# Rotating keys and queries by transfers, with a new order in the window attention and an earlier fetch of the distances' table

## What is computed

```python
q = rms_norm(q, q_norm); k = rms_norm(k, k_norm)      # per head, gain of 64
q, k = rope(q, positions), rope(k, positions)         # halves of 32: x1*cos - x2*sin, x2*cos + x1*sin
logits = q @ k.T * 64 ** -0.5                         # masked to the last 128 keys
p = softmax over [logits, sink of the head]           # the sink takes part in the sum only
y = (p @ v) @ w_out
```

## Time and profile before

| | |
|---|---|
| median of 3 timed runs | 2091.65 us |
| the profiled execution | 2096.21 us, span 2094.3 us |
| mean granted TensorE clock | 0.995 |
| PE (matmuls) busy | 2067.1 us, 99% |
| PEld (weight loads, beside PE) | 1740.9 us, 83% |
| DVE (VectorE) busy | 1779.1 us, 85% |
| ACT (ScalarE) busy | 1400.0 us, 67% |
| POOL (GpSimd) busy | 59.6 us, 3% |
| moved by DMA | 565.92 MB, 270 GB/s over the span |

### The profile page before, as it was taken

One profiled execution on the slowest core, in us unless ns is written; L12 is line 12 of the kernel. 1 busy time (PEld: TensorE's weight loads), 2 busy tenths in 40 slices (PEclk: granted clock), 3 DMA queues, 4 the chain that ended last, 5 costly groups with the idle time before them and its releaser, 6 DMA issues. The chain is left out here.

```text
span 2094.3 us, 27806 instructions
## 1 busy us (share of the span) xinstructions
PE 2067.1 (99%) x10830; PEld 1740.9 (83%) x10830; DVE 1779.1 (85%) x2358; ACT 1400.0 (67%) x1855; POOL 59.6 (3%) x58
## 2 busy tenths in 40 slices
PE   9999999999999999999999999999999999999999
PEld 8878888878888888888888888879988888778887
DVE  6776768789999999999999999988878888788887
ACT  5654547568888888888888888867745446565544
POOL 0011002001000000000000000000000000000000
PEclk9999999999999999999999999999999999999999
DMA  9537764659999999999999999954446555346552
GB/s 312 181 121 271 233 209 151 219 199 395 394 395 395 395 395 383 385 380 386 371 393 374 388 372 378 394 202 141 144 159 227 196 181 149 81 154 222 183 197 102
DMA packets 291275, 565.92 MB, mean 270 GB/s; under 512 B 13596, under 2 KB 120224, under 8 KB 290896
## 3 DMA queue, kind: packets, MB, share of 16 engines
q1 hardware_dynamic: 284480, 537.13, 71.8%
q0 software_dynamic: 5792, 23.78, 3.1%
q10 hardware_dynamic: 864, 3.15, 0.4%
HBM read 555.10 MB, written 12.59 MB: 271 GB/s over the span
## 5 line engine op out<-in xcount | busy, mean ns | idle before, releaser
L505 DVE TENSOR_TENSOR wl<-raw,wh 128x1024 fp32r<-128x1024 f32 x626 | 756.2, 1242 | 99.9 <-ACT wh L497 95.5
L497 ACT ACTIVATE wh<-raw 128x1024 fp32r<-128x1024 f32 x626 | 640.9, 1053 | 154.1 <-PE psum L542 61.7
L505 DVE TENSOR_TENSOR wl<-arena,wh 128x1024 fp32r<-128x1024 f32 x384 | 456.7, 1222 | 37.6 <-ACT wh L497 32.6
L497 ACT ACTIVATE wh<-arena 128x1024 fp32r<-128x1024 f32 x384 | 403.9, 1062 | 84.7 <-PE psum L542 82.5
L540 PE MATMUL psum<-wh,xhl 128*128 128x512 f32 (+1 forms) x1136 | 449.5, 396 | 1.8 <-DVE wl L505 0.9
L542 PE MATMUL psum<-wh,xhl 128*128 128x512 f32 (+1 forms) x1136 | 441.5, 389 | 0.0
L541 PE MATMUL psum<-wl,xhl 128*128 128x512 f32 (+1 forms) x1136 | 440.6, 388 | 0.0
L532 PE MATMUL psum<-xhl,wh 128*128 128x512 f32 x980 | 349.4, 396 | 0.0
L540 PE MATMUL psum<-wh,yh 128*128 128x512 f32 x752 | 295.6, 393 | 1.0 <-DVE yl L1714 1.0
L542 PE MATMUL psum<-wh,yl 128*128 128x512 f32 x752 | 293.0, 390 | 0.0
L541 PE MATMUL psum<-wl,yh 128*128 128x512 f32 x752 | 292.6, 389 | 0.0
(11 more groups left out here) (455 smaller groups left out, 2078.1 us busy)
## 6 DMA issues: line engine op xcount, KB each, us to landing
arena<-in_moe_g SPq DMA_DIRECT2D x72, 1024.0 KB, 8.8
arena<-in_moe_u SPq DMA_DIRECT2D x72, 1024.0 KB, 8.5
raw<-in_moe_d SPq DMA_DIRECT2D x64, 1024.0 KB, 8.8
arena<-in_moe_d SPq DMA_DIRECT2D x48, 1024.0 KB, 8.3
raw<-in_ff_up SPq DMA_DIRECT2D x48, 1024.0 KB, 5.2
raw<-in_moe_g SPq DMA_DIRECT2D x40, 1024.0 KB, 8.1
raw<-in_moe_u SPq DMA_DIRECT2D x40, 1024.0 KB, 9.2
raw<-in_ff_down SPq DMA_DIRECT2D x24, 1024.0 KB, 5.4
```

What stands on the lines that cost most here:

```text
L497: A.activation(unit_made(s, i)[0], raw_half(s, i), ACT.Copy).then_inc(*s.w_hi.tick(i))
L505: V.tensor_tensor(lo, raw_half(s, i), hi.bitcast(F), SUB).then_inc(*s.w_lo.tick(i))
```

## The change

Four parts. (1) GpSimd fetches the bias table and the one-hot matrix at once, without the wait for the first piece of x; the clock holder after the first piece does two turns instead of three. (2) The rotation is done by transfers between partitions of SBUF: when ScalarE has copied a block to `QB`, it waits for its own copy and issues four DMAs of 32 partitions each (64 KB) that write the swapped halves to `T4`. `rope` is gone from TensorE. Sign and gain are now a column `ROT_GAIN`, made by two one-column matmuls (`rotated_gains`) at the section's beginning, and VectorE's `sines` multiplies the swapped block by this column and the sines, in place. `copied` for the later blocks also waits until the earlier contents are used up. (3) `maxima` can do the small steps of two units together. (4) The order is changed: on TensorE `turned(3)` goes ahead of `sums(1)`; on ScalarE `turned(3)`, the copies `newer` and the high halves move; on VectorE `masked(4)`, `masked(6)`, `rows(0, 1)` go ahead of `scales(1)`, `maxima(4)` and `maxima(6)` ahead of unit 13's low half, `older(7)` and `maxima(5, 7)` ahead of `normal(4, 6)`, and `rows(1, 0)` ahead of `normal(7)`.

```diff
--- before.py
+++ after.py
@@ -320,6 +320,7 @@
     back_in = [sig(f"back{n}_landed", 16) for n in range(4)]
     added_in = [sig(f"added{n}_landed", 16) for n in range(3)]
     added_out, added_back = sig("added_stored", 16), [sig(f"added_back{l}", 16) for l in range(2)]
+    rotated = {(n, i): sig(f"rotated{n}{i}", 16) for n in range(3) for i in range(1 if n == 2 else 2)}
     res_in, ln_in, tz_in, out_done = sig("x_landed", 16), sig("ln_landed", 16), sig("tz_landed", 16), sig("out_landed", 16)
 
     def C(name):
@@ -1086,7 +1087,7 @@
                     if c == 3:
                         i.then_inc(*pe.tick(("unit", u), f"{st}.in{n}"))
                 if (m, c) == (0, 0):
-                    hold_clock(7, 3, STILL[:, 0:P], STILL)
+                    hold_clock(7, 2, STILL[:, 0:P], STILL)
                 if (m, c) == (0, 1):
                     T.wait_ge(*distances_in.of("all"))
                     T.matmul(take(4)[0:4, 0:384], S("relb")[0:32, :], C("oh")[0:32, :], start=True, stop=True
@@ -2921,12 +2922,12 @@
     WP, WPO = [ar(9728 + 512 * n, 4, 128) for n in range(4)], [ar(11776 + 512 * n, 4, 128) for n in range(2)]
     WD = ar(8704, 256)
     NSK = SC[:, 960:976]
-    ROT = [SC[:, 640:768], SC[:, 768:896]]
+    ROT_GAIN = SC[:, 640:642]
     RV, RR, RW1, RW2, RW, RW64 = (SC[:, 448 + 2 * n:450 + 2 * n] for n in range(6))
     LG_BANKS = [(5,), (2, 3), (1,), (6, 7), (0,), (1, 5), (4,), (0, 4)]
     PT_BANK = [5, 6, 1, 7, 1, 0, 5, 4]
     AV_BANK = [[5, 5], [1, 5]]
-    Q_BANKS, RO_BANKS, SS_BANK = {2: (0,), 0: (2, 3), 1: (0, 4)}, {2: (6,), 0: (6, 7), 1: (0, 4)}, {2: 4, 0: 4, 1: 1}
+    Q_BANKS, RO_BANKS, SS_BANK = {2: (0,), 0: (2, 3), 1: (0, 4)}, {2: (6,), 0: (6, 7), 1: (2, 3)}, {2: 4, 0: 4, 1: 1}
 
     def win_at(n):
 
@@ -2971,14 +2972,12 @@
             x.then_inc(*pe.tick(f"wi.ss{n}"))
             empties(SS_BANK[n], (dve, f"wi.ss{n}"))
 
-        def rope(n):
-            for i, b in enumerate(RO_BANKS[n]):
-                take(b)
-                T.wait_ge(*act.of(f"wi.qc{n}{i}"))
-                T.wait_ge(*dve.of("wi.rot"))
-                T.matmul(bk(b), ROT[n == 2], flat(QB[:, 2 * i:2 * i + 2, :]), start=True, stop=True
-                         ).then_inc(*pe.tick(f"wi.ro{n}"))
-                empties(b, (dve, f"wi.ro{n}"))
+        def rotated_gains():
+            ps = take(6)
+            for i, n in enumerate(("aqn", "akn")):
+                x = T.matmul(ps[:, i:i + 1], C("rot"), S(n), start=True, stop=True)
+            x.then_inc(*pe.tick("wi.rot"))
+            empties(6, (dve, "wi.rot"))
 
         def spread_keys():
             ps = take(5)
@@ -3037,16 +3036,15 @@
             x.then_inc(*pe.tick(f"wi.av{g}{t}"))
             empties(b, (dve, f"wi.x{g}{t}"))
 
+        rotated_gains()
         project(2, 0, by_blocks("nm1"))
         project(2, 1)
         project(0, 0)
-        rope(2)
         project(0, 1)
         sums(2)
         project(0, 2)
         project(0, 3)
         spread_keys()
-        rope(0)
         sums(0)
         project(1, 0)
         logits(0, 2)
@@ -3056,12 +3054,11 @@
         project(1, 3)
         turned(0)
         turned(2)
-        rope(1)
         weigh(0, 0)
         turned(1)
         logits(4, 6)
+        turned(3)
         sums(1)
-        turned(3)
         weigh(0, 1)
 
         def turn_first():
@@ -3086,9 +3083,14 @@
         def copied(n, i):
             A.wait_ge(*pe.of(f"wi.p{n}{i}"))
             if n != 2:
-                A.wait_ge(*pe.of(f"wi.ro{0 if n else 2}"))
+                A.wait_ge(*rotated[0 if n else 2, 0].of("all"))
                 A.wait_ge(*dve.of(f"wi.c0{i}" if n else "wi.c20"))
+                A.wait_ge(*dve.of(f"wi.q{0 if n else 2}"))
             A.activation(QB[:, 2 * i:2 * i + 2, :], heads(bk(Q_BANKS[n][i]), 2), ACT.Copy).then_inc(*act.tick(f"wi.qc{n}{i}"))
+            A.wait_ge(*act.of(f"wi.qc{n}{i}"))
+            for a in range(4):
+                A.dma_start(T4[32 * a:32 * a + 32, 2 * i:2 * i + 2, :], QB[32 * (a ^ 1):32 * (a ^ 1) + 32, 2 * i:2 * i + 2, :]
+                            ).then_inc(*rotated[n, i].tick("all"))
 
         def squared(n, i):
             if n != 2:
@@ -3153,24 +3155,22 @@
         squared(1, 1)
         weighed(0, 0)
         turned(1)
+        turned(3)
         hi_to(main, U + 15)
-        turned(3)
-        hi_to(main, U + 16)
         weighed(0, 1)
         hi_to(main, U + 17)
+        newer(5)
         soft(4)
-        newer(5)
+        newer(7)
+        soft(6)
         hi_to(main, U + 18)
-        soft(6)
-        newer(7)
-        hi_to(main, U + 19)
         soft(5)
         turned(4)
         turned(6)
-        hi_to(main, U + 20)
+        hi_to(main, U + 19)
         soft(7)
         weighed(1, 0)
-        hi_to(main, U + 21)
+        hi_to(main, U + 20)
         turned(5)
         turned(7)
         hi_to(main, un["wi.o2"][0] + NU)
@@ -3187,11 +3187,12 @@
                                    CS[:, 0, :].unsqueeze(1).to_broadcast([P, 2, 256]), MUL, MUL).then_inc(*dve.tick(f"wi.c{n}{i}"))
 
         def sines(n):
-            V.wait_ge(*pe.of(f"wi.ro{n}"))
+            V.wait_ge(*dve.of("wi.rot"))
             m = 2 * len(RO_BANKS[n])
-            for i, b in enumerate(RO_BANKS[n]):
-                V.tensor_tensor(T4[:, 2 * i:2 * i + 2, :], heads(bk(b), 2), CS[:, 1, :].unsqueeze(1).to_broadcast([P, 2, 256]), MUL
-                                ).then_inc(*dve.tick(f"wi.ro{n}"))
+            for i in range(len(RO_BANKS[n])):
+                V.wait_ge(*rotated[n, i].of("all"))
+                V.scalar_tensor_tensor(T4[:, 2 * i:2 * i + 2, :], T4[:, 2 * i:2 * i + 2, :], ROT_GAIN[:, (n == 2):(n == 2) + 1],
+                                       CS[:, 1, :].unsqueeze(1).to_broadcast([P, 2, 256]), MUL, MUL).then_inc(*dve.tick(f"wi.ro{n}"))
             V.wait_ge(*dve.last())
             q = RP[:, win_at(n), :]
             V.tensor_tensor(q, q, T4[:, 0:m, :], ADD).then_inc(*dve.tick(f"wi.q{n}"))
@@ -3222,19 +3223,25 @@
                 V.copy_predicated(WE[u % 4][:, 2 * i:2 * i + 2, :], C("tri").bitcast(I32).unsqueeze(1).to_broadcast([P, 2, P]),
                                   heads(bk(b), 2)[:, :, 0:P]).then_inc(*dve.tick(f"wi.l{u}"))
 
-        def maxima(u):
-            nm, _, sk, x = soft_cols(u)
-            gr, t, L = u // 2, u % 2, WE[u % 4]
+        def soft_pair(*us):
+            a = 64 + 16 * us[0]
+            return (SC[:, a:a + 64].rearrange("p (u n j) -> p u n j", u=2, j=4)[:, 0:len(us), n, :] for n in range(4))
+
+        def maxima(*us):
+            t, gr = us[0] % 2, us[0] // 2
             _, r, _, _ = win_scales(gr // 2)
-            r4 = r[:, 8 * t:8 * t + 8].rearrange("p (j g) -> p g j", g=2)[:, gr % 2, :]
-            V.wait_ge(*dve.of(f"wi.l{u}"))
-            V.tensor_reduce(x, L, AX, MAX, negate=True).then_inc(*dve.tick())
+            r4 = r[:, 8 * t:8 * t + 8].rearrange("p (j g) -> p g j", g=2)[:, gr % 2:gr % 2 + len(us), :]
+            ns = NSK[:, 4 * gr:4 * gr + 4 * len(us)].rearrange("p (u j) -> p u j", j=4)
+            nm, _, sk, x = soft_pair(*us)
+            for n, u in enumerate(us):
+                V.wait_ge(*dve.of(f"wi.l{u}"))
+                V.tensor_reduce(x[:, n, :], WE[u % 4], AX, MAX, negate=True).then_inc(*dve.tick())
             V.wait_ge(*dve.last())
             V.tensor_tensor(x, x, r4, MUL).then_inc(*dve.tick())
             V.wait_ge(*dve.last())
-            V.tensor_tensor(nm, x, NSK[:, 4 * gr:4 * gr + 4], MIN).then_inc(*dve.tick())
+            V.tensor_tensor(nm, x, ns, MIN).then_inc(*dve.tick())
             V.wait_ge(*dve.last())
-            V.tensor_tensor(sk, nm, NSK[:, 4 * gr:4 * gr + 4], SUB).then_inc(*dve.tick(f"wi.m{u}"))
+            V.tensor_tensor(sk, nm, ns, SUB).then_inc(*dve.tick(*[f"wi.m{u}" for u in us]))
 
         def begin(u):
             if u % 2:
@@ -3279,8 +3286,8 @@
         for a in range(2):
             V.tensor_scalar(NSK.rearrange("p (g a b) -> p g a b", g=4, a=2)[:, :, a, :],
                             sn.rearrange("p (g b a) -> p g b a", g=4, b=2)[:, :, :, a], -1.0, None, MUL).then_inc(*dve.tick("wi.nsk"))
-        V.tensor_scalar(ROT[0], C("rot"), S("aqn"), None, MUL).then_inc(*dve.tick())
-        V.tensor_scalar(ROT[1], C("rot"), S("akn"), None, MUL).then_inc(*dve.tick("wi.rot"))
+        V.wait_ge(*pe.of("wi.rot"))
+        V.tensor_copy(ROT_GAIN, bk(6)[:, 0:2]).then_inc(*dve.tick("wi.rot"))
         lo_to(main, U + 7)
         cosines(2, 0)
         lo_to(main, U + 8)
@@ -3307,23 +3314,27 @@
         lo_to(main, U + 13)
         sines(1)
         normal(3)
+        part_older(1)
         rows(0, 0)
-        part_older(1)
+        masked(4)
         part_older(3)
+        masked(6)
+        rows(0, 1)
         scales(1)
-        rows(0, 1)
+        maxima(4)
+        maxima(6)
         lo_to(main, U + 14)
-        begin(4)
+        older(5)
         lo_to(main, U + 15)
-        begin(6)
-        begin(5)
+        older(7)
+        maxima(5, 7)
         lo_to(main, U + 16)
```

(7 more changed lines are left out.)

## The result

| | before | after |
|---|---|---|
| median of the timed runs | 2091.24 us (4) | 2111.45 us (4: 2109.67 to 2113.9) |
| ratio | | 1.0088, 95% interval 1.0076 to 1.0101 |
| the profiled execution | 2096.21 us, span 2094.3 us | 2109.67 us, span 2107.9 us |
| mean granted TensorE clock | 0.995 | 0.991 |

The two medians differ by 20.2 us, which is 1.0%; the ratio in the table and its interval put the cost at 0.8 to 1.0%. The time lies outside the range of the prediction.

What follows compares the result with a forecast made beforehand. PE, busy 99% of the span, bounds the kernel, losing time only where it waits or runs at half clock. Start -3.1 and window section +6.5 give +3.4 us on 2091.65: 2095.0 us, range 2086 to 2101.

Steps and rivals of the forecast that it cites:

- The start: Kernel start: earlier table and one clock-holder turn less give -3.1 us, between -1.7 and -3.4.
- From the first copy to the first weighted sum: Window section's first part: weighted sum starts at 1813.3 us instead of 1817.37, -4.0 us.
- An issue on ScalarE: Window section: 0.35 us an issue, 1.55 us a block with its copy wait, 7.8 in all; bounds 0.1 and 0.5.
- The landing: Rotated blocks in the window section: 2.1 us, up to 2.8 us under weight traffic.
- a sign of being wrong: Window section's transfers: landing after 4 us or more was listed as showing the prediction wrong.
- From the first weighted sum on: Window section's later part: VectorE's new order takes the gain back; section 2.3 us later at full clock, +6.5 with two falls.
- the two falls: TensorE's clock falls behind two of four pauses of 3.0 to 4.0 us, making the section 5.4 to 8.4 us later.
- the low half: Unit 13, projection's second step: PE waits 3.0 us for VectorE, starting at 1829.6 us against 1831.98.
- the divided weights: Window attention: PE waits 3.1 us for normal(4, 6) and 3.4 us before turning unit 7.
- Three or four falls: Rival, window section: clock falls at three or four pauses, section +9 to +11, total about 2099 us; chance 0.18.
- Transfers one after another: Rival, queries' second half: a block's four transfers run serially, about 6 us more, 2101 us; chance 0.02.
- From the profiled run to the median: Whole kernel: profiled run lies 4.56 us above the timed median 2091.65; the +3.4 us was added to that median.

Runs made afterwards that it cites:

- the new order alone: Start's change, after's order on all three engines and joint maxima, against before; rotation stays matmuls, no transfers: 2101.82 us, 1.0043 of before.
- three places mended: Kernel after with three places of VectorE's order put back (low half of unit 13, normal(4, 6), normal(7) earlier): 2101.67 us, 1.0044 of before.
- the kernel with the other banks: Kernel before with the start's change and the third rotation writing banks 2 and 3 instead of 0 and 4: 2091.02 us, 0.9986 of before.
- one issue and the order mended: Kernel after with one 256 KB transfer a block (swap of the halves left out) and VectorE's order mended in three places: 2089.45 us, 0.9982 of before.
- The later groups: Follow-up runs in three groups of four rows, each on its own chip with the kernel before beside them: before's medians 2093.42, 2093.11 and 2093.23 us.
- weights held: Kernel after with two of SP's weight loads held until the rotated block ahead of them had landed: 2113.47 us, 1.0099 of before.
- the best kernel: Kernel before with the start's change, the third rotation on banks 2 and 3, and unit 13's low half moved behind the queries' sines: 2088.50 us, 0.9975.
- the kernel with the other banks and the new order mended: Matmul rotation on the other bank pair, start's change, new order with VectorE's three places mended, no transfers, against before: 2093.74 us, 0.9995.

## Why the prediction was wrong

The step that failed is the price of a transfer on ScalarE: both of its terms, the issue and the landing, were too small, and with them the path through ScalarE to TensorE's first weighted sum. A second miss is in how the profiled run was carried over to the median.

- **The start: right.** L1093 at 10.10 us (10.3 forecast), no wait, the clock at 1.00. L1243 (before L1242) began at 86.50 us instead of 89.88, 3.4 us earlier for the forecast 3.1. The first copy came 2.8 us earlier with the rotated gains of 0.4 us ahead of it, but that sum is no sharper test: the first copy lies anywhere from 1771.4 to 1774.9 us in the profiled runs with this start. The small fetch was issued at 1.98 us, not 1.1, and landed 3.6 us later, not 6.7; the two errors went opposite ways. What the timed medians leave open stands above.
- **From the first copy to the first weighted sum: wrong, and this is the miss.** Forecast -4.0 us. Before it took 1817.37 - 1776.8 = 40.6 us; after it took 1820.74 - 1774.0 = 46.7: **+6.1**. Two terms of the sum were too small.
  - *An issue on ScalarE.* I took 0.35 us from the only row there was, of 512 KB loads, and 0.5 as the upper end from SP's. It was 0.61, so 2.45 to 2.53 us a block instead of 1.4 (1.55 with the wait for its own copy), beyond my bound. ScalarE around the first queries, in order of time:

```profile
1783.88 0.60 ACT L3089 ACTIVATE arena<-psum 128x512 f32<-128x512 f32 x1 [3.47 <-DVE arena L3198]
1784.51 2.45 ACTq L3092 DMA_DIRECT2D arena<-arena  x4
1789.39 0.59 ACT L3089 ACTIVATE arena<-psum 128x512 f32<-128x512 f32 x1
1790.01 2.44 ACTq L3092 DMA_DIRECT2D arena<-arena  x4
1792.50 0.60 ACT L3098 ACTIVATE arena<-psum 128x512 f32<-128x512 f32 x1 [2.52 <-issue]
```

  The square ends at 1793.1 and the sums of squares begin at 1793.24: PE's 4.5 us wait, put down to another engine, ended with this square. I had 1.9 us for it. For the copy of the turned weights I had 4.0 us and it was 6.3: L3126 began at 1819.52 us, right behind four issues that took from 1817.03 to 1819.47.
  - *The landing.* I took 2.1 us and at most 2.8 under weight traffic. In quiet stretches it was 2.0, but 5.1 for the keys' block and 6.7 for a queries' block. I had 1.6 us of waiting for the keys' block; VectorE waited 5.6. The first row above shows what the keys' cost: ScalarE waits 3.5 us for VectorE's L3198, which waited for them. The prediction named this as a sign of being wrong: transfers landing after 4 us or more.
- **From the first weighted sum on: right in mechanism, and in size partly by luck.** Forecast +6.5 - (-4.0) = +10.5 us, of which 4.2 for the two falls. Measured: 1889.0 - 1820.74 = 68.3 against 1875.4 - 1817.37 = 58.0, **+10.3**. The waits were as laid out: 2.6 us for the low half (3.0), 5.9 in two for the divided weights (6.5). The runs with the new order alone (+9.8) and with three places mended (-8.3) show the cause. The luck is in the clock: two falls began in this part and a third, from 1818 us, reached into it, behind a wait that I had too short.
- **The number of falls: two forecast, four came** (from about 1791, 1818, 1849 and 1859 us). They go with PE's waits of 4.5, 6.3, 2.9 and 3.1 us; the wait of 2.6 us had none. The first two stand in the part with the misjudged waits. The step that took pauses over 3 us as the condition was too simple: a wait of 1.8 us went before a fall in the kernel with the other banks, and waits of 2.4 and 1.8 us in the one with one issue and the order mended, at the same place, before none.
- **The rivals.** "Three or four falls" came at the right count but at 2099, since it had the same terms. "Transfers one after another" was the dearest of them (2101), still 10 us short, and not the way: the landings overlapped (2.0 us for each of four), and it was the issues and the weights that took the time.
- **From the profiled run to the median.** The profiled runs differ by 13.5 us, the medians by 20.2. The profiled run of before lay 4.56 us above its median (4.97 above that of the table), and I carried the difference over unchanged; the profiled run of after lay 1.78 us below its own. Before's clock was 0.66 over 1400 to 1410 us where the other kernels' was mostly 0.83. The later groups show that this is spread and no offset: over their 64 runs the kernel before has 2089.33 to 2097.57 us, median 2093.25, with a mean clock that differs from run to run. This term was worth 6.7 us and had no range of its own. With the 10.1 us of the first part it is the miss of 16.5 us, but for 0.3 us.

## What to carry to other kernels

A transfer in place of a matmul is paid on the engine that issues it: count the issues, price them by a row of the same shape or leave a factor of two, and look at what is queued behind them on that engine. Its landing has to be priced with the DMA share of the very stretch. Before a wait for a buffer is bought off with other work, look for a free bank; and where an order by hand is changed, ask of each piece that VectorE does whether TensorE needs it sooner than what stands ahead of it.

## What the hardware showed that I had not expected

- An issue on ScalarE's queue took 0.34 us for the 512 KB loads, 0.47 for 256 KB from SBUF to SBUF on 128 partitions, and 0.61 for 64 KB on 32 partitions: smaller, and dearer. GpSimd took 0.50 for the same 64 KB.
- Landings of 64 KB issued by ScalarE took 1.9 to 3.0 us at DMA shares up to 0.77 and 4.3 to 7.1 us at 1.02 and more (kernels after and weights held); issued by GpSimd, up to 8.8 us at 1.11.
- The clock. In the kernel with one issue and the order mended it stayed up; both rows are PE's, in order of time, and with the stretch below them:

```profile
1808.40 1.08 PE L3029 MATMUL psum<-arena 128*64 128x512 f32 x4 [2.38 <-ACT arena L3124]
1811.91 1.16 PE L3005 MATMUL psum<-arena 64*128 64x128 f32 x16 [1.85 <-DVE SC L3267]
```

```profile
1814.00:1817.00 3.00, 3.00 (x21) 1.74 (x20) 1.67 (x3) 1.24 (x2) 0.00 (x0) 1.00 0.01 3
```

With less waiting, 1.24 and 0.78 us, the best kernel had 0.68 in that stretch. What tells the two apart wasn't settled. It isn't the order of the matmuls: the kernel with the other banks and the new order mended has the same one, and the same wait (1.83 us) ahead of the same scores, and its profiled run had 0.68 and then 0.50 there, while four of its twelve timed runs had the mean clock of a run with fewer falls.
